# A two-block network on one core: a new order for the delta rule and the attention of the first block

## The reference, cut to what matters

```
h = rms_norm(x, pre_mix_norm)
q, k, v, qkv, z, a, b = split(h @ w_in)            # 8 attention heads, 8 delta-rule heads, 64 wide
o_att = attention(q, k, v) with relative bias      # S = 256 is one block: plain causal softmax
qkv   = silu(causal_depthwise_conv(qkv, conv_w))   # 4 taps
qd, kd, vd = split(qkv);  qd, kd = l2_normalize(...)
beta = sigmoid(b);  g = -exp(A_log) * softplus(a + dt_bias)
per chunk of tokens, per head:
    decay = exp(where(causal, gcum_i - gcum_j, -inf))
    m = strict_lower((kd*beta) @ kd.T * decay)
    u, w = inverse(I + m) @ (vd*beta, kd*beta*exp(gcum))
    o, state = delta rule step with state
o_gdn = rms_norm(o) * norm_w * silu(z)
x = x + rms_norm(concat(o_att, o_gdn) @ w_out)
x = x + rms_norm(relu(h @ w_up)**2 @ w_down)       # then a second block: conv, retention, gated FFN
```

## Time and profile before

| what | value |
|---|---|
| median of 3 runs | 972.07 us |
| the profiled execution | 973.27 us, its span 971.5 us |
| PE busy | 929.9 us (96%) |
| DVE busy | 594.3 us (61%) |
| ACT busy | 465.3 us (48%) |
| POOL busy | 91.4 us (9%) |
| granted TensorE clock, mean | 0.990 of 2.4 GHz |
| from HBM | 157.91 MB, 165 GB/s over the span |

### The profile page before, as it was taken

One profiled execution on the slowest core, in us unless ns is written; L12 is line 12 of the kernel. 1 busy time (PEld: TensorE's weight loads), 2 busy tenths in 40 slices (PEclk: granted clock), 3 DMA queues, 4 the chain that ended last, 5 costly groups with the idle time before them and its releaser, 6 DMA issues.

```text
span 971.5 us, 12793 instructions
## 1 busy us (share of the span) xinstructions
PE 929.9 (96%) x5492; PEld 812.0 (84%) x5492; DVE 594.3 (61%) x667; ACT 465.3 (48%) x547; POOL 91.4 (9%) x93
## 2 busy tenths in 40 slices
PE   6998869999999999999999999999999999999997
PEld 5998658887788888789998988888888778888885
DVE  5679784376755566767684546455456555555564
ACT  5865345546444443564534232632535455454442
POOL 2005331001000000010030330101100000000000
PEclk9998999999999999999999999999999989999999
DMA  8551420032555445554465434444445535545441
GB/s 315 200 185 65 173 95 26 23 130 91 200 215 210 174 173 188 203 204 163 171 217 188 165 135 179 173 173 171 166 147 189 195 112 213 206 173 198 170 164 44
DMA packets 24217, 159.81 MB, mean 165 GB/s; under 512 B 3240, under 2 KB 3512, under 8 KB 5856
## 3 DMA queue, kind: packets, MB, share of 16 engines
q1 hardware_dynamic: 21600, 152.58, 42.5%
q0 software_dynamic: 2272, 6.24, 1.9%
q10 hardware_dynamic: 288, 0.17, 0.1%
HBM read 157.91 MB, written 2.63 MB: 165 GB/s over the span
## 4 chain that ended last, share of the span: by engine, by line
PE 82%; DVE 10%; ACT 5%; issue 2%; POOL 1%; DMA 0%; DVEq 0%; POOLq 0%; ACTq 0%
PE banks L471 30%; PE banks L413 18%; PE banks L439 14%; PE banks L442 7%; PE banks L496 3%; DVE t_wl L1395 2%; PE banks L392 2%; PE banks L916 1%; ACT t_wh L984 1%; PE banks L714 1%; PE banks L554 1%; DVE t_cout L1411 1%; PE banks L737 1%; ACT t_hold L992 1%; DVE t_gs L1407 1%
## 5 line engine op out<-in xcount | busy, mean ns | idle before, releaser
L1395 DVE TENSOR_TENSOR t_wl<-t_raw,t_wh 128x2048 fp32r<-128x2048 f32 (+1 forms) x144 | 327.8, 2300 | 150.7 <-ACT t_wh L984 149.7
L984 ACT CAST t_wh<-t_raw 128x2048 fp32r<-128x2048 f32 (+1 forms) x144 | 269.0, 1901 | 34.6 <-PE banks L413 20.0
L413 PE MATMUL banks<-t_hx,t_wh 128*128 128x256 f32 x1232 | 225.8, 286 | 0.4 <-ACT t_cin L1100 0.4
L413 PEld LDWEIGHTS banks<-t_hx,t_wh 128*128 128x128 f32 x1232 | 194.5, 194 | 2.5 <-DVE t_hx L1411 1.3
L439 PE MATMUL banks<-t_hx,t_wh 128*128 128x512 f32 x576 | 182.4, 398 | 1.9 <-DVE t_hx L1411 1.9
L413 PE MATMUL banks<-t_hx,t_wl 128*128 128x256 f32 x616 | 175.3, 285 | 0.0
L442 PEld LDWEIGHTS banks<-t_hx,t_wl 128*128 128x128 f32 x576 | 109.1, 189 | 25.7
L413 PEld LDWEIGHTS banks<-t_hx,t_wl 128*128 128x128 f32 x616 | 119.3, 194 | 0.0
L442 PE MATMUL banks<-t_hx,t_wl 128*128 128x256 f32 x576 | 113.9, 279 | 0.0
L471 PE MATMUL banks<-t_wh,t_hx 128*128 128x512 f32 x320 | 102.0, 397 | 0.0
L439 PEld LDWEIGHTS banks<-t_hx,t_wh 128*128 128x128 f32 x576 | 90.3, 191 | 4.1 <-DVE t_hx L1411 2.3
(11 more groups left out here) (294 smaller groups left out, 1264.8 us busy)
## 6 DMA issues: line engine op xcount, KB each, us to landing
t_raw<-in_W SPq DMA_DIRECT2D x143, 1024.0 KB, 4.9
skew<-scr POOLq DMA_DIRECT2D x1, 1536.0 KB, 15.9
t_x<-in_x SPq DMA_DIRECT2D x2, 512.0 KB, 4.9
t_T<-skew POOLq DMA_DIRECT2D x8, 128.0 KB, 2.4
out<-t_xt SPq DMA_DIRECT2D x4, 256.0 KB, 2.1
t_tab<-in_tab POOLq DMA_DIRECT2D x1, 640.0 KB, 6.6
t_raw<-in_W SPq DMA_DIRECT2D x1, 512.0 KB, 7.1
t_T<-skew POOLq DMA_DIRECT2D x8, 64.0 KB, 3.1
```

The source lines that it names most:

```text
L413: m = e.matmul(bank[b][:, c * S:c * S + S], W[w][:, h, k * 128 * nt + c * 128:k * 128 * nt + c * 128 + 128], H[a][:, k, :], start=first, s ...
L984: e.copy(M.wh[:, h, 0:n], M.raw[:, r, 0:n]).then_inc(q.sem, q.tick(("hi", i)))
L1395: e.tensor_tensor(M.wl[:, h, 0:n], M.raw[:, r, 0:n], M.wh[:, h, 0:n].bitcast(F32), ALU.subtract).then_inc(q.sem, q.tick(("lo", i)))
```

## The change

The order of the units becomes: conv 0 to 5, z, qk 0 to 3, va. On each engine the parts of the mixer move with it:

- The `decay` matmuls stand behind conv 3, and DVE's sixteen instructions on them behind the taps of conv 3. They now take the minimum with a table `M.cap` (0 where allowed, -1e30 elsewhere), so that POOL's multiply of `dU` with the causal mask goes away.
- Transposes of queries and keys stand in the middle of conv 5, in banks 0 to 3; those of the values in the middle of z.
- The norms of queries and keys: POOL takes the power -0.5 (`root`) in place of ACT's square root and DVE's reciprocal; keys are scaled before queries. The same for the output norm (`so`).
- `kT` stands behind qk 0, `KQ` behind qk 1, the hand-out behind qk 3. `va` comes last, in the fixed banks 2 and 3, with the first two softmax scores between and behind its neighbours.
- POOL's multiplies by `nstrict` and by `near` and its addition of the identity go to DVE, whole.
- The sum over the 16 blocks of `near` is four additions of halves in place of two reductions.
- A head's probabilities are normalised on DVE (`att_norm`) behind the softmax of the next head.
- ACT copies the transposed inverse (`X`) before the exponential of head 1. The numbers of attention steps beside the four levels become (3,2), (3,2), (3,2), (2,2) in place of 2 and 2 each.
- ACT's first SiLU comes a unit later; POOL's first bias loads (`load_T`) come earlier.

```diff
 def plan():
     u += [("B", "w_in", 1536 + 256 * i) for i in range(6)]
+    u += [("C", "w_in", 3072, k) for k in (0, 4)]
     u += [("B", "w_in", 256 * i) for i in range(4)]
     u += [("C", "w_in", 1024, k) for k in (0, 4)]
-    u += [("C", "w_in", 3072, k) for k in (0, 4)]
...
+BEFORE = 3
+BESIDE = ((3, 2), (3, 2), (3, 2), (2, 2))
...
 # tensor
-                b_unit(("conv", u), x_in, AC, ("cin", u))
+                b_unit(("conv", u), x_in, AC, ("cin", u), mid=queries_and_keys if u == 5 else None)
...
+            c_block("z", x_in, [(AC, ("zz", t)) for t in range(2)], lambda: token_major(2))
             b_unit(("qk", 0), x_in, AC, ("qk", 0))
...
+            att(1)
+            c_block("va", x_in, [(AC, ("va", t)) for t in range(2)], lambda: att(1), (2, 3))
...
-            att(3)
+            att(BEFORE)
...
-                    q.wait_ge(PO, "A")
+                    q.wait_ge(DV, "A")
...
 # scalar
+            att(1)
+            next_unit()
             next_unit()
             for c in range(2):
-                q.wait_ge(PE, ("z", c))
-                e.activation(M.zz[:, c, :], bank[at["z", c]][:], ACT.Silu).then_inc(q.sem, q.tick(("zz", c)))
+                q.wait_ge(PE, ("va", c))
+                e.copy(M.va[:, c, :], bank[at["va", c]][:]).then_inc(q.sem, q.tick(("va", c)))
...
 # vector
+                            stt(M.dU[:, s, :], bank[b][:, i * 128:i * 128 + 128], M.gcum[:, s:s + 1], M.cap,
+                                ALU.subtract, ALU.min, ("dU", g))
...
+            tt(M.AT, M.dU[:], rep(M.nstrict, 16), ALU.mult, "dS")
...
-            for c in range(2):
-                q.wait_ge(*((PO, ("near", 0)) if c == 0 else (q, ("near", 1))))
-                e.tensor_reduce(M.ab_[:, 8 * c:8 * c + 8], ...
+            tt(M.XT, M.AT, rep(M.near, 16), ALU.mult, "near")
+            q.wait_ge(q, "near")
+            blocks = M.XT.rearrange("p s (b i) -> p s b i", i=BASE)
+            for n in (8, 4, 2):
+                tt(blocks[:, :, 0:n, :], blocks[:, :, 0:n, :], blocks[:, :, n:2 * n, :], ALU.add, ("fold", n))
+                q.wait_ge(q, ("fold", n))
+            tt(M.ab_, blocks[:, :, 0, :], blocks[:, :, 1, :], ALU.add, "ab_")
...
                     if kind == "scores":
                         att_scores(h)
+                        if h:
+                            att_norm(h - 1)
+                    elif kind == "turn" and h == 7:
+                        att_norm(h)
...
+            tt(M.AT, M.AT, rep(ident[:], 16), ALU.add, "A")
+            next_unit()
+            att(1)
+            att(BEFORE)
...
 # gpsimd
-            tt(M.dU[:], M.dU[:], rep(M.triu, 16), ALU.mult, "dU")
-            tt(M.AT, M.dU[:], rep(M.nstrict, 16), ALU.mult, "dS")
+            load_T(0)
+            load_T(1)
+            q.wait_ge(DV, "rn1")
+            root(M.rn, "rn")
...
-            tt(M.AT, M.AT, rep(ident[:], 16), ALU.add, "A")
```

More of the change, by code:

```diff
@@ L267, in memory @@
         M.kd = tm[:, 0, 0:512]
-        M.triu, M.nstrict, M.ones, M.near, M.same, delta = (tab[:, i, :] for i in range(6))
+        M.triu, M.nstrict, M.ones, M.near, M.same, delta, M.cap = (tab[:, i, :] for i in range(7))
         M.delta = delta[:, 0:BASE]
@@ L615, in tensor @@
[L615 to L617 removed]
+                elif u == 3:
+                    for g in range(4):
+                        b = take(("decay", g), g)
+                        opened(b)
+                        for i in range(4):
+                            s = 4 * g + i
+                            m = e.matmul(bank[b][:, i * 128:i * 128 + 128],
+                                         M.graw[:, s:s + 1].broadcast_to([128, 128]), M.triu, start=True, stop=True)
+                        m.then_inc(q.sem, q.tick(("decay", g)))
+                        drain(b, DV, ("dU", g))
```

243 lines of the change are left out of this document (106 added, 137 removed).

## The result

The changed kernel takes 969.83 us (median of 20 runs, 967.71 to 972.07), the kernel before 973.2 us (median of 20 runs beside them, 971.24 to 977.33). The ratio is 0.9968, with a 95% interval of 0.996 to 0.9976: 0.3% faster, about 3.1 us. The profiled execution has a span of 968.7 us, before 971.5. The 20 runs of the kernel before have a median 1.1 us above that of the three runs from which the forecast started.

What follows compares the result with a forecast made beforehand. TensorE's waits for VectorE and the lowered clock were taken as the bound: idle 15.3 to 13.2 us saves 2.1, clock returns 5.0, less 3.1 for a new clock fall: 4.0 saved, 972.07 to 968.1 us; range 963.0 to 972.6.

Steps and rivals of the forecast that it cites:

- New wait of the third transposes: After the first half of z, TensorE waits 1.7 us for the last SiLU; sixteen masked decay instructions take 4.2 to 6.6.
- What goes: Key transposes: 2.77 + 0.36 us of waits and 2.6 of clock gone; GpSimd's root taken as 0.6 us, hidden.
- Sums by halves: Before the hand-out: additions take 2.6 us against 3.91; the 5.38 us wait and 2.2 of clock go, margin 1.4.
- What is late next: Between hand-out and first level: TensorE waits 1.6, 3.5, 1.1 and 2.2 us; first level starts at 131.1.
- In the levels: Deferred normalisation costs waits of 1.4 us at turn 2 and 1.7 at turn 7, none at turns 3 to 6.
- Rival C: Deferred normalisation bares turns 3 to 6, 2.2 us each, 8.8 together: 976.9 us; chance 0.11.
- Output norm: GpSimd's root takes 0.6 us against 0.5, hidden by the mixing matmuls, at worst 0.5 us each if bare.
- The clock: Between 119.0 and 131.1 us TensorE is nearly empty; the clock may fall there, 3.1 us taken for it.
- the three terms: Low-clock cost before: key transposes 5.61 less 0.36 against 2.66, hand-out and half unit 2.2, next unit 0.3; together 5.0 us.
- Rival A: Clock stays at 2.4 GHz between 119 and 131 us: saving 7.1, 965.0 us; chance 0.20.
- Rival B: VectorE later than worked out, 1 to 2 us wait returns, clock falls twice: saving 0 to 2, 971 us; chance 0.19.

Runs made afterwards that it cites:

- uncap: Changed kernel with decay differences bounded by zero and GpSimd's triangle product back: 976.15 us, ratio 1.0039 to the kernel before.
- best: Changed kernel with earlier divisions, inverse's start first, sum of squares behind the taps, output root on ScalarE: 964.54 us, 0.9917 to the kernel before.
- cap_only: Kernel before with only the decay mask added and GpSimd's triangle product removed: 969.17 us, ratio 0.9968.
- fold_only: Kernel before with only the block sums made by four additions of halves instead of two reductions: 975.10 us, ratio 1.003.
- norm_now: Changed kernel with each head divided by its sum in its own turn again: 964.96 us, ratio 0.9922 to the kernel before.
- again: Changed kernel run once more, unaltered: 968.98 us, ratio 0.9965 to the kernel before.
- fold_late: Kernel before with sums by halves and GpSimd's identity addition held back until VectorE's spread: 976.22 us, ratio 1.0029.

## Why the prediction was right, step by step

The forecast was 968.1 us from a kernel at 972.07, that is 4.0 us less; measured are 3.1, inside the range. Of the 1.7 us between 968.1 and 969.83, 1.1 is the median of the kernel before, which is 973.2 over 20 runs. The mechanism was right, the closeness is in part luck. Up to the states the forecast saved 2.1 us of idle and 1.9 of clock; measured are 3.3 of idle and 0.9 of busy time, 4.2 together. Behind the states 2.4 us were lost, and 1.0 won by the first unit's step: 2.8 in the profile. By its steps:

1. *New wait of the third transposes*: forecast 1.7 us, measured 0.98. The sixteen decay instructions with the mask took 4.22 us, the lower end of the bounds. The wait is real and ends on ScalarE's last SiLU.
2. *What goes*: right in mechanism, and uncap shows it: 2.77 us before the key transposes and the clock at 88 to 91 are gone, 0.37 is left. The root's size was wrong by nine times (0.6 taken, 5.62 measured), above even the upper bound of 4.6: a power on GpSimd costs by the column, and one column says nothing on that. The root was hidden, as said, but by less than was thought (it ends at 68.95 us and is read at 70.38); in best it wasn't. The price of the clock behind the transposes, 2.6 us, is near what cap_only gave back there, 2.1.
3. *Sums by halves*: 2.7 us for 2.6; the spread ends at 102.3 for 103.5, TensorE comes without a wait at 103.95 for 104.9. What the step left out: fold_only shows that the halves are a loss of 2.7 us where GpSimd's addition stands beside them. They are harmless in the change only because that addition went, and with a margin of 1.6 us at the hand-out their 1.2 us were not needed. Rows 6 had that addition's neighbours in them, the reductions that it didn't hold up.
4. *What is late next*: 1.04, 3.34, 0.93, 2.24 us for 1.6, 3.5, 1.1, 2.2. The first level was to start at 131.1 and did at 131.7; without the 1.0 us at the start it would be 132.7, and 1.4 of the 1.6 us are the clock in the turns and the score.
5. *In the levels*: 1.36 and 1.67 us at turns 2 and 7 for 1.4 and 1.7, none at turns 3 to 6. Rival C fell, but norm_now shows that the same deferral cost 4.0 us at turns 0, 1, 2 and 7, whose waits the forecast had counted (1.1, 2.2, 1.4 and 1.7) and taken as given.
6. *Output norm*: taken as hidden, at worst 0.5 us each. The roots of 8 columns took 1.67 and 1.64 us for 0.6, and TensorE got a wait of 0.6.

The clock: it fell where it was said, behind the waits, from 126.2 to 136.3 us. The 3.1 us taken for it lie between the 3.6 of the first profile and the 2.4 of `again`. Its price before was put too high: 5.0 us (the three terms add up to 5.1), where half of TensorE's busy time at 0.50, from 87.7 to 94.1 and from 125.1 to 128.5 us, is 4.4. States: 184.14 for 184 to 186, with 1.0 us of luck at the kernel's start in it; without it, 185.1. Behind the states 2.4 us were lost that the forecast hadn't: 0.6 by step 6, and the rest by the clock, at 404 to 424 us in this execution and at other places in the next. Why the clock falls at one of these places in one execution and not in the next stays open.

Rival A (clock stays up) is out by the 0.50 at 128 to 136. Rival B (VectorE late, waits at the key transposes and hand-out) is out: the margin at the hand-out was 1.6 us. But with GpSimd's product back (uncap) or a late root (best) it is just what happens.

## What to carry to other kernels

Before work is given to VectorE or GpSimd, ask for every product or addition of over a microsecond what the other has beside it and of which kind each is: here one GpSimd product or addition of 2048 columns made one VectorE instruction beside it some 4 us longer at four different places, and the kernel 3 to 7 us slower (cap_only, uncap, fold_only, fold_late). It held up additions, products, a short scaling and a short copy alike, and only the reductions not. An edit that shortens an instruction (four additions for two reductions) can be a loss because of its kind. And when waits of one chain are spread over an engine that works in fixed order, move the chain itself ahead: its order on VectorE was worth 3.5 us, the place of the division 4.0, the whole change with its many moves 3.1.

## What the runs showed of the hardware

- GpSimd's power costs by the column: 0.55 us for 1, 1.67 for 8, 5.62 for 32 columns, some 0.16 us each.
- The block between VectorE and GpSimd goes both ways, by who is first. GpSimd's identity addition takes 4.53 us beside VectorE's reductions, 5.56 when VectorE's first halving runs, 6.54 behind a low part; its root 5.62, and 7.62 behind a low part. VectorE's 2.28 us low part takes 6.64, its 0.23 us copy 4.08.
- GpSimd's root, once it runs, holds nothing up. In the changed kernel it runs from 63.33 to 68.95 us, and VectorE's six taps, which read two tensors from SBUF, take their usual 2.46 us beside it:

```profile
63.15 2.46 DVE L1412 SCALAR_TENSOR_TENSOR t_cout<-t_cin,t_small,t_cout 128x256 f32<-128x256 f32 x6
68.17 2.29 DVE L1396 TENSOR_TENSOR t_wl<-t_raw,t_wh 128x2048 fp32r<-128x2048 f32 x1 [2.56 <-ACT t_wh L988]
```

  GpSimd's next product starts at 68.94, so it was at work until then. Beside a product such instructions are held up, as the low part of uncap was; why a power differs is open.
- Small instructions alternate rather than stand still: in the changed kernel, 70.4 to 76.8 us, VectorE's products of 512 columns took 1.42 to 1.79 us each beside GpSimd's of the same size, and two of them 1.28 us together at 78.93, when GpSimd was idle.
